# Delta-rule build and attention norms: evictions taken between the inversion's masks, the gate product ahead of the norm

## What is computed

```
proj = rmsnorm(x) @ w_in
out_lru = (rg_lru(...)      * silu(lru_z)) @ w_lru_out
out_nsa = (attention(q,k,v) * silu(nsa_z)) @ w_nsa_out     # q, k: rmsnorm, then rope
o_dn    = rmsnorm(gated_delta(...), dn_o_norm)
out_dn  = (o_dn             * silu(dn_z))  @ w_dn_out
y = (mg0*out_lru + mg1*out_nsa + mg2*out_dn) @ w_out;  x = x + y
```

## Time and profile before

| | us |
|---|---|
| median of 3 runs | 1844.32 (1844.13 to 1846.75) |
| the profiled execution, own time | 1844.07 |
| its span, first to last instruction | 1842.20 |
| PE matmul busy | 1773.8 (96%) |
| DVE busy | 970.0 (53%) |
| ACT busy | 518.8 (28%) |
| POOL busy | 91.0 (5%) |
| TensorE clock granted | 0.999 of full |

### The profile page before, as it was taken

How to read it: one execution, slowest core, us unless ns; L and a number is a source line. 1 busy time by engine, 2 the same in 40 slices (tenths; PEclk the granted TensorE clock), 3 DMA queues, 4 the chain that set the end, 5 groups by cost and what they waited for, 6 DMA issues and landing times.

```text
span 1842.2 us, 28682 instructions
## 1 busy us (share of the span) xinstructions
PE 1773.8 (96%) x10974; PEld 1263.1 (69%) x10974; DVE 970.0 (53%) x2306; ACT 518.8 (28%) x1165; POOL 91.0 (5%) x133
## 2 busy tenths in 40 slices
PE   7999999999999999999999999989999999999999
PEld 5777687775655577776467777878756555777763
DVE  2749654544756456433137596555357664645321
ACT  3142412115266522100212424020143664211000
POOL 0000201002200000000000002010112000000000
PEclk9999999999999999999999999999999999999999
DMA  6312411123530146544042232020245211564421
GB/s 214 103 46 69 103 41 31 40 64 123 141 94 24 38 121 184 163 157 145 0 164 71 67 80 86 25 46 25 63 138 156 64 35 41 161 176 118 160 74 40
DMA packets 196525, 170.01 MB, mean 92 GB/s; under 512 B 49248, under 2 KB 186898, under 8 KB 195942
## 3 DMA queue, kind: packets, MB, share of 16 engines
q1 hardware_dynamic: 192164, 150.11, 28.1%
q0 software_dynamic: 4064, 18.03, 3.0%
q10 hardware_dynamic: 162, 0.05, 0.0%
HBM read 153.66 MB, written 21.71 MB: 95 GB/s over the span
## 4 chain that ended last, share of the span: by engine, by line
PE 77%; DVE 14%; issue 3%; SPq 2%; ACT 2%; DMA 1%; ACTq 0%; DVEq 0%
PE PS L947 51%; PE PS L876 5%; DVE arena L1899 3%; DVE arena L1824 3%; PE PS L1328 2%; PE PS L1341 2%; PE PS L1167 1%; PE PS L1149 1%; PE PS L1397 1%; SPq L664 1%; PE PS L1169 1%; PE PS L1053 1%; DVE ws L1830 1%; PE PS L1181 1%; SPq L671 1%
## 5 line engine op out<-in xcount | busy, mean ns | idle before, releaser
L947 PE MATMUL PS<-hT,ring 128*128 128x288 f32 x2384 | 631.7, 410 | 11.3 <-DVE arena L2009 3.1
L947 PEld LDWEIGHTS PS<-hT,ring 128*128 128x128 f32 x2384 | 439.5, 190 | 141.3 <-issue 11.7
L947 PE MATMUL PS<-tt,ws 128*128 128x288 f32 x736 | 205.9, 413 | 13.9 <-DVE arena L1827 5.0
L947 PE MATMUL PS<-zs,owr 128*128 128x288 f32 x768 | 208.0, 412 | 4.0 <-DVE sg L1830 2.3
L947 PEld LDWEIGHTS PS<-tt,ws 128*128 128x128 f32 x736 | 132.9, 190 | 57.7 <-DVE sg L1957 8.0
L947 PEld LDWEIGHTS PS<-zs,owr 128*128 128x128 f32 x768 | 138.4, 190 | 49.2 <-issue 13.2
L876 PE MATMUL PS<-con,arena 128*128 128x128 f32 (+5 forms) x950 | 146.1, 280 | 14.9 <-DMA arena<-in_nsa_k_norm 10.8
L876 PEld LDWEIGHTS PS<-con,arena 128*128 128x128 f32 (+5 forms) x950 | 109.5, 140 | 73.0 <-issue 43.6
L1827 DVE TENSOR_TENSOR sg<-PS,sg 128x288 f32<-128x288 f32 x140 | 63.9, 457 | 135.3 <-PE PS L947 129.6
L947 PE MATMUL PS<-arena 128*128 128x512 f32 (+1 forms) x320 | 124.8, 593 | 2.1 <-DVE sg L1957 2.1
L947 PE MATMUL PS<-tt,ring 128*128 128x288 f32 x368 | 103.6, 415 | 6.3 <-DVE sg L1827 6.3
(11 more groups left out here) (314 smaller groups left out, 2092.6 us busy)
## 6 DMA issues: line engine op xcount, KB each, us to landing
ring<-in_w_in SPq DMA_DIRECT2D x54, 1024.0 KB, 5.5
arena<-in_cache_nsa_kv SPq DMA_DIRECT2D x128, 192.0 KB, 2.7
ring<-in_w_in SPq DMA_DIRECT2D x32, 256.0 KB, 4.6
arena<-in_state_nsa_win SPq DMA_DIRECT2D x32, 256.0 KB, 3.3
arena<-in_cache_nsa_kv SPq DMA_DIRECT2D x128, 64.0 KB, 1.8
arena<-in_w_out SPq DMA_DIRECT2D x4, 2048.0 KB, 8.4
out_win_sample<-in_state_nsa_win POOLq DMA_DIRECT2D x2, 4032.0 KB, 23.0
arena<-in_x_prompt SPq DMA_DIRECT2D x8, 512.0 KB, 5.6
```

Source lines behind the costliest of these rows:

```text
L947: ins = mm(to, w, x, start=start, stop=stop, skip_group_check=True)
```

## The change

In the build, DVE now forms B, Q, B first, then takes the finished units, then X, takes again, and then Y. As X now reads bank 3 last, PE waits ahead of a second tile's products for the Y of the group's first tile (`i_xm`) in place of its B (`p_b`).

In the norms, ACT takes the first product of the first merge pair and forms Silu of the delta rule's gate right behind the squares of o; Silu of the attention's gate goes behind the second copy of transposed keys. DVE multiplies that gate into the raw outputs, in two halves, ahead of the norms (in `zs`, not in `dc`), and the norm of o is applied to the product; the product that stood behind the norms is gone, `dn_ok` is only signalled. PE fills 20 ahead of its wait for `bm_ok` 10, in place of 16 behind it. Two takings in the rotation of the keys reach one unit further.

```
@@ PE, build
                         if li:
-                            pe.wait_ge(s["p_b"], past["p_b"] + k)
+                            pe.wait_ge(s["i_xm"], past["i_xm"] + n_ix + 1)
@@ PE, norms
                 dense_to(u0 + U_MG0)
+                fill(20, u0 + U_MG2)
                 pe.wait_ge(s["bm_ok"], past["bm_ok"] + 10)
-
-                fill(16, u0 + U_MG2)
                 pe.wait_ge(s["qk_ok"], past["qk_ok"] + 1)
@@ ACT, norms
                     A(dc[:, 4 + n], dc[:, n], ACT.Square).then_inc(s["sq_ok"], 1)
+                take_to(u0 + U_MG0 + 1)
+                act.wait_ge(s["pa"], taken(u0 + U_MG0, "A"))
+                act.wait_ge(s["pv"], taken(u0 + U_MG0, "V"))
+                A(zs[:, 8:12], zs[:, 8:12], ACT.Silu).then_inc(s["silu_ok"], 1)
                 take_before("b_pe", 4 + DN_H)
...
                 root_of("q", rs7[:, 0])
-                take_to(u0 + U_MG0)
-                act.wait_ge(s["pa"], taken(u0 + U_MG0, "A"))
-                act.wait_ge(s["pv"], taken(u0 + U_MG0, "V"))
-                A(zs[:, 8:12], zs[:, 8:12], ACT.Silu).then_inc(s["silu_ok"], 1)
-                A(zs[:, 4:8], zs[:, 4:8], ACT.Silu).then_inc(s["silu_ok"], 1)
-
...
                         .then_inc(s["kt_e"], 1)
+                    if k == 1:
+                        A(zs[:, 4:8], zs[:, 4:8], ACT.Silu).then_inc(s["silu_ok"], 1)
@@ DVE, build
                         mul(dc[:, 0:4, t:t + n], dc[:, 0:4, t:t + n], tmp["E"][:, li, :, 0:n])
+                        dve.wait_ge(s["p_d"], past["p_d"] + k + 1)
+                        B, Q = tmp["B"][0:n, li, :, 0:n], kq[0:n, li, :, P:P + n]
+                        link(mul(B, bank4(3, n, n), D))
+                        mul(Q, bank4(4, n, n), D)
+                        mul(B, bank4(5, n, n), B).then_inc(s["p_b"], 1)
+                        take_before("p_g", 4 * k + 3)
                         X, Y = (xy(li, n, x) for x in range(2))
...
                         link(add(X[:, :, 0:n:2], X[:, :, 0:n:2], rep(ident[0:n, 0:n:2], DN_H)))
-                        dve.wait_ge(s["p_d"], past["p_d"] + k + 1)
-                        B, Q = tmp["B"][0:n, li, :, 0:n], kq[0:n, li, :, P:P + n]
-                        link(mul(B, bank4(3, n, n), D))
-                        mul(Q, bank4(4, n, n), D)
-                        mul(B, bank4(5, n, n), B).then_inc(s["p_b"], 1)
+                        take_before("p_g", 4 * k + 4)
                         dve.wait_ge(s["p_b"], past["p_b"] + k + 1)
@@ DVE, norms
+                take_before("ms_ok", 3)
+                dve.wait_ge(s["silu_ok"], past["silu_ok"] + 5)
+                for n in range(2):
+                    if n:
+                        take_before("ms_ok", 4)
+                    gated = zs[:, 8 + 2 * n:10 + 2 * n]
+                    link(mul(gated, gated, dc[:, 2 * n:2 * n + 2]))
                 for h in range(2):
-                    times_roots("o", h, dc[:, 0:4], prm("on")).then_inc(s["bm_ok"], 1)
+                    times_roots("o", h, zs[:, 8:12], prm("on")).then_inc(s["bm_ok"], 1)
...
                 dve.wait_ge(s["bm_ok"], past["bm_ok"] + 10)
-                dve.wait_ge(s["silu_ok"], past["silu_ok"] + 5)
-                mul(zs[:, 8:12], zs[:, 8:12], dc[:, 0:4]).then_inc(s["dn_ok"], 1)
+                dve.sem_inc(s["dn_ok"], 1)
...
-                        take_to(normed + 2)
+                        take_to(normed + 3)
                     link(mul(x, x, rep(C("cos"), m - n)))
...
-                        take_to(normed + 3)
+                        take_to(normed + 4)
                     add(x, x, y).then_inc(s["qk_ok"], 1)
```

## The result

The changed kernel takes **1830.2 us** (median of 4 runs, 1828.69 to 1831.33) against 1845.2 of the kernel before on the same chip: ratio 0.9917, interval 0.9905 to 0.9929. The forecast was 1825.8 with a range of 1820 to 1834. The profiled execution has a span of 1827.8 (own time 1829.64), 14.4 less than before, where I forecast 18.3 less.

The account below looks back on a forecast made before the run. TensorE (PE) was taken as the bound, busy 270.65 of 285 us. Per layer 7.0 + 2.8 - 0.25 - 0.4 = 9.15, twice 18.3, off 1844.07 gave 1825.8 us, range 1820 to 1834.

Parts of the forecast that it names:

- it doesn't do what it says: Rival on PE's waits: the evictions are not what ends them; time about 1843 us, no chance of its own given.
- Build, 7.0: Build: PE's waits for late evictions mostly go, a gain of 7.0 us per layer, bounds 4.0 to 8.9.
- Y on the path: Rival in the build: takings ahead of Y hold up the inversion; build gives 4.0 per layer, 1831.8 us, chance 0.14.
- Layer 2 counts like layer 1: Both layers: PE works the same 270.65 us in each, so whatever is found in one counts twice.
- Norms, 2.8: Norms: 1.69 + 1.44 + 0.45 - 0.8 = 2.8 us gained per layer, bounds 0.5 to 4.7.
- I take 0 to 0.2: Norms: PE's wait if the keys' swapped rows land late, taken as 0 to 0.2 us; 2.1 at latest landing.
- second rival: Norms: keys' rows land late or Silu costs over 0.8; norms give 0.5, 2.3 less per layer, 1830.4 us, chance 0.12.
- The gate product's move: Norms: DVE's two halves, 2.56 us together, fit in its 5.44 idle and cost nothing; without that cover up to 2.6.
- Loop, 0.65 lost: Slot loop: 0.25 us lost per layer at the last slots and 0.4 by the new phase, the latter bounded -1.5 to 3.
- The rival of 3 per layer: Rival in the slot loop: it gives part of the gain back, 3 us per layer, time 1831.0 us, chance 0.10.
- that of 11.0: Rival in the slot loop: four trains of weight sums precede awaited reductions, 11.0 us per layer, 1847.0 us, chance 0.03.
- Nothing behind the loop: Behind the loop: SP's cached keys wait for `qk_ok` 2 and move with the rest, so a loss of 0.

Follow-up runs that it names:

- e4_notake: The changed kernel without the second taking of the build, the one ahead of Y: median 1829.6 us, ratio 0.9919.
- e9_hold: The changed kernel with SP holding its next two output weight loads until the keys' swapped rows have landed: median 1828.3 us, ratio 0.9910.
- e8_fill: The changed kernel with 16 fills ahead of PE's wait for `bm_ok` 10 in place of 20: median 1831.6 us, ratio 0.9929.
- e5_phase: The changed kernel without the four fills behind the last piece ahead of the slot loop: median 1828.6 us, ratio 0.9910.

## Why the prediction was right or wrong

- **PE's waits, ended by late evictions, are what the change takes back: right.** The build alone gives -13.9 of the span's -14.4 (-15.0 between M0 and M1, as in the changed kernel), and the order without the takings gives next to nothing, so "it doesn't do what it says" fell.
- **Build, 7.0: right** at 6.80 in layer 1. Of its parts, 0.4 was forecast at each of the two long waits and 0.21 shown measured. At the single tile I had 0.6 on the inversion's path; 0.76 was shown, so that this tile gains nothing instead of 0.2. `e4_notake` confirms the mechanism (three weight sums ahead of Y) at 0.82. PE's new wait for Y cost nothing, as forecast. The rival "Y on the path" named the mechanism, but its price was 3 per layer. That price doesn't follow from its terms either: 1.35 and twice 2.05 are 5.45, of which 0.9 was already in the sum.
- **Layer 2 counts like layer 1: wrong by 1.38**, in the change's favour. "The same 270.65" of busy time in both layers hid it: a matmul at the lower clock counts as busy for longer, so the second window held the same busy time and less work. The 0.99 in the second of the earlier trace rows was the sign that I passed over; the distance from M0 to M1 shows it at once. For the same reason the layers are 910.39 apart at M0, and the 911.8 given at the start holds only behind the build. Without this 1.38 the span had fallen by 13.0; that it came nearer to the forecast is luck.
- **Norms, 2.8: mis-sized, 1.52 and 1.28 measured.** The Silu cost 0.33 at the Tanh and 0.38 at the squares' sums, 0.71 for the forecast 0.8, and ACT's timeline has the table load at 429.10 and the Silu at 430.39, as soon as the load ends: by the drain that the Trainium skill (ScalarE: Activation LUTs, What ACT_TABLE_LOAD costs) adds it would have begun 1.38 later. The trace disagrees with the page here too. The two waits of 1.53 and 1.28 went, and the third fell by 0.44 for the forecast 0.45. The step that failed is "I take 0 to 0.2" for the keys' rows. The estimate put their landing 4.8 behind POOL's first issue; it was 6.3. I had taken the 2.8 of a median transfer and not seen the two loads on SP's queue that are issued among them. The trace of before had the answer: the longest of the four transfers took 4.7 to land, and in both kernels the last one was issued 1.5 behind the first. And I looked for the price at the wrong place: the rotated keys had slack from the four fills, but product 6, which is taken behind the sine, had none. That is 0.72 and 0.95 of PE. `e9_hold`, with the landing at 4.5, shows it. That is the second rival's mechanism at a smaller price than its 2.3. In the sum of shown waits the norms won 1.82 in layer 1 (1.53 + 1.28 + 0.44 - 0.71 - 0.72); the other 0.3 down to the measured 1.52 is in no shown wait. Forecast was 0.16 of hidden time taken back at each wait that went, and nothing for the new ones.
- **The gate product's move: right as to its cover, wrong as to its worth.** On DVE it stands at 432.84, with 3.29 of idle time behind it. But it is worth 0.72 and 0.48, since DVE waited 1.79 and 2.02 for the rows in the time it won. And that the wait for the rotated keys goes is the four fills' work: in `e8_fill` it is 1.74.
- **Loop, 0.65 lost: mis-sized, 0.94.** Forecast as 0.25 for the last slots and 0.4 for the phase. In shown waits it was 0.20 at a copy of values in the last slots (PE at 633.79) and 1.06 at one reduction, and the stretch lost 0.94 of it. With the old phase, in `e5_phase`, both are gone. The rival of 3 per layer fell, and so did that of 11.0: one train of weight sums out of four met a reduction that PE waited for, and it cost 1.06.
- **Nothing behind the loop: wrong, 0.56 and 0.80.** "It moves with the rest" holds for the start of SP's train (9.27 behind M3 in both kernels), not for its length, and PE waits at its fifth group.

## What to carry to other kernels

Where one engine both evicts a saturated TensorE's products and prepares its next operands, take the finished products between the parts of the preparation, and stop where what hangs on a taking (here three weight sums) is longer than the slack of the last part. Moving a fill from one wait to another is a loan: count what it covers and what it uncovers, in a run with the fills alone undone. Ask of a short transfer on the path which loads another queue issues beside it; a hold of those loads cost one wait instruction and gave more than moving an operation of 2.56 us.

## What the hardware showed unexpectedly

- A wait of TensorE of 1.74 to 2.54 us is followed in some executions by the lower clock level for about 3 us, at a cost of 1.4 to 1.6 us, and in others by none; the same program showed both in its two layers.
- Four swaps of rows within SBUF (54 KB each) landed at most 4.5 us behind the first issue with no other load of SP beside them, and let DVE start 6.3 and 6.5 behind it beside two loads of 256 KB; issued by ACT in place of POOL, beside the same loads, 7.5 and 6.9 behind it.
- SP took 16.7 to 18.0 us for each 16 issues of the cached keys and values. From the first issue to the end of the fifth group the time differed by up to 1.5 us between kernels that were the same there.
